# Softmax rows of first and local attention turned by VectorE blocks and DMA, value products behind gates, experts' first slots fetched early

## What is computed

```python
# layers 0, 1
p = softmax(concat([scores_a, sink_col], -1))[..., :-1]
ya = einsum('bnkgqj,bnjkd->bnqkgd', p, va) @ w_proj_a      # first attention, "a"
yb = neighbourhood_attn(qb, kb, vb, rel_bias) @ w_proj_b   # "b"
x = x + (sigmoid(ga) * ya + sigmoid(gb) * yb) @ w_out
# layers 2, 3
y_a = dilated_attention(q_a, k_a, v_a, rel_bias)           # local attention in 256 tokens, "c"
y_m = sigmoid(z_m) * norm(mlstm_chunkwise(q_m, k_m, v_m, i_pre, log_f))
merged = g_a * (y_a @ w_br_a) + g_m * (y_m @ w_br_m)       # g_*: sigmoid(x @ w_gate + b_gate)
y = sum(gate[..., e] * swiglu(x, w13[e], w2[e]) for e in range(8))   # layer 3
```

## Time and profile before

| | before |
|---|---|
| median of 3 timed runs | 2236.96 us (2236.05 to 2237.69) |
| profiled execution | 2238.39 us |
| its span, first to last instruction | 2237.0 us |
| mean granted TensorE clock | 0.998 |
| PE busy | 2217.7 us, 99% |
| DVE busy | 1760.3 us, 79% |
| ACT busy | 1364.5 us, 61% |
| POOL busy | 167.5 us, 7% |
| DMA | 611.39 MB, mean 273 GB/s |

### The profile page before, as it was taken

The page is one execution under the profiler, slowest core; times in us unless marked ns, Lnnn a source line. Parts: engine busy times, 40 slices in busy tenths (PEclk is TensorE's granted clock), DMA queues, the critical chain, the costliest instruction groups (busy, mean ns, idle before and its releaser), DMA issues.

```text
span 2237.0 us, 30263 instructions
## 1 busy us (share of the span) xinstructions
PE 2217.7 (99%) x12156; PEld 1904.7 (85%) x12156; DVE 1760.3 (79%) x2253; ACT 1364.5 (61%) x1764; POOL 167.5 (7%) x231
## 2 busy tenths in 40 slices
PE   9999999999999999999999999999999999999997
PEld 7998888998888999888899887888888888888886
DVE  7976656977564588665678898999999998989898
ACT  5654444655443454444455577777777777877775
POOL 3100111300120000211100010000000000000001
PEclk9999999999999999999999999999999999999999
DMA  8455764546763535776625699999999999999996
GB/s 279 151 191 212 240 233 154 176 170 215 246 235 132 185 132 208 245 236 205 226 93 187 249 349 406 386 380 388 376 382 382 386 370 386 373 392 360 390 372 251
DMA packets 104163, 611.39 MB, mean 273 GB/s; under 512 B 24056, under 2 KB 25384, under 8 KB 34896
## 3 DMA queue, kind: packets, MB, share of 16 engines
q1 hardware_dynamic: 80496, 568.76, 67.3%
q0 software_dynamic: 9872, 31.12, 4.0%
q10 hardware_dynamic: 13648, 9.50, 1.6%
HBM read 591.07 MB, written 18.62 MB: 273 GB/s over the span
## 4 chain that ended last, share of the span: by engine, by line
PE 96%; DVE 3%; DMA 1%; ACT 0%; issue 0%; SPq 0%; POOL 0%; DVEq 0%
PE bank L491 28%; PE bank L493 28%; PE bank L492 28%; PE bank L488 8%; DVE wl L1662 2%; PE bank L768 1%; PE bank L721 1%; PE bank L521 1%; DMA spare<-in_ws 1%; DMA raw<-in_ws 0%; PE bank L816 0%; PE bank L1088 0%; DVE TU L1873 0%; DVE EL L1689 0%; ACT wh L1189 0%
## 5 line engine op out<-in xcount | busy, mean ns | idle before, releaser
L1662 DVE TENSOR_TENSOR wl<-raw,wh 128x1024 fp32r<-128x1024 f32 x698 | 819.9, 1223 | 219.9 <-ACT wh L1189 216.7
L1189 ACT ACTIVATE wh<-raw 128x1024 fp32r<-128x1024 f32 x704 | 704.3, 1052 | 331.1 <-PE bank L493 295.2
L491 PE MATMUL bank<-wh,GH 128*128 128x512 f32 x896 | 352.8, 394 | 0.0
L493 PE MATMUL bank<-wh,GL 128*128 128x512 f32 x896 | 349.3, 390 | 0.0
L492 PE MATMUL bank<-wl,GH 128*128 128x512 f32 x896 | 348.8, 389 | 0.0
L1662 DVE TENSOR_TENSOR wl<-spare,wh 128x1024 fp32r<-128x1024 f32 x264 | 309.8, 1221 | 26.8 <-ACT wh L1189 25.3
L1189 ACT ACTIVATE wh<-spare 128x1024 fp32r<-128x1024 f32 x264 | 264.2, 1054 | 61.0 <-PE bank L493 56.9
L491 PE MATMUL bank<-HH,wh 128*128 128x256 f32 x832 | 239.6, 288 | 0.1
L492 PE MATMUL bank<-HL,wh 128*128 128x256 f32 x832 | 235.3, 283 | 0.0
L493 PE MATMUL bank<-HH,wl 128*128 128x256 f32 x832 | 235.2, 283 | 0.0
L491 PE MATMUL bank<-wh,HH 128*128 128x512 f32 (+1 forms) x600 | 223.4, 372 | 0.0
(11 more groups left out here) (319 smaller groups left out, 3537.1 us busy)
## 6 DMA issues: line engine op xcount, KB each, us to landing
raw<-in_ws SPq DMA_DIRECT2D x352, 1024.0 KB, 6.6
spare<-in_ws SPq DMA_DIRECT2D x132, 1024.0 KB, 7.1
more<-in_ws SPq DMA_DIRECT2D x48, 1024.0 KB, 5.0
scratch_blocks<-TB POOLq DMA_DIRECT2D x30, 256.0 KB, 2.9
TURNED<-scratch_blocks POOLq DMA_DIRECT2D x36, 128.0 KB, 4.8
once<-in_ws SPq DMA_DIRECT2D x4, 1024.0 KB, 11.4
scratch_parts<-Y POOLq DMA_DIRECT2D x7, 512.0 KB, 8.5
REL<-in_relb ACTq DMA_DIRECT2D x4, 768.0 KB, 13.3
```

Source lines behind the costliest of these rows:

```text
L491: T.q.matmul(o, l[0], r[0], start=start, stop=False)
L493: return T.q.matmul(o, l[1], r[0], start=False, stop=stop)
L1189: A.q.activation(sets[c % NSET][0][:, half * i:half * i + half], raws[stream.place[n]][:, half * i:half * i + half], ACT.Copy).then_inc(*h ...
L1662: V.q.tensor_tensor(wl[:, half * i:half * i + half], raw[:, half * i:half * i + half], wh[:, half * i:half * i + half].bitcast(f32), ALU.s ...
```

## The change

The rows of "a" and "c" are no longer turned by PE. `v_even_blocks` takes the place of `v_even`: the product by the reciprocal writes PT with the rows arranged in blocks of 32 columns, and two block transposes of 128 x 1024 (128 x 512 for tile 0 of "c") bring them back to LB[t]. `g_turn_p`, on POOL's queue, writes LB[t] to DRAM in two pieces and reads it back in four strided pieces into other buffers: QT (the queries of "a" are through) and PT for "a", LB[t] for "c". `t_block_outputs` reads them in blocks of 32 columns. For "b" the old way stays, but its turned rows land in QBT (by `turned_piece`), and the first half of its queries in QB0.

The value products move behind gates: in layers 0 and 1 tile 0's behind gate 5 and tile 1's behind the second half of gate 6; in layers 2 and 3 tile 0's keep their place behind the first half of gate 2, and tile 1's stand behind the second half of gate 3, whose first half moves ahead of mq and mk. On DVE, `v_gate(l, 1)` of layers 0 and 1 moves behind the block work of tile 0 and the scores of tile 1; ACT's order changes with it. The closing product of a convolution becomes `v_conved`, which stands one convolution later.

For the experts a fifth once buffer is added, and the five are filled as their memory comes free in layer 3 instead of at the router's norm; the load of BIAS moves from `a_router` to behind expert 1's first products, on ACT's queue. The diff, with unchanged lines left out (left out as well: the new semaphores, the declarations of RZX and of the DRAM buffer, the list of five once names and the removal of BIAS's old load):

```diff
@@ -358,8 +360,9 @@
...
-        for i, a in enumerate((0, 2048, 4096, 14336)):
-            raws[f"once{i}"] = at(f"once{i}", a, SLOT)
+        raws["once0"] = nc.alloc_sbuf_tensor_at("once0", [128, SLOT], f32, offset=arena_at + 4 * 22016)
+        for i, a in enumerate((4096, 0, 2048, 14336)):
+            raws[f"once{i + 1}"] = at(f"once{i + 1}", a, SLOT)
...
@@ -412,6 +415,13 @@
...
+        QB0 = U[:, 6656:7168]
+        def turned_rows(a, t):
+            return {"a": (QT[:, 0:2048], PT[:, :]), "c": LB}[a][t]
+        def turned_piece(a, c):
+            return QBT[c // 2][:, 512 * (c % 2):512 * (c % 2) + 512] if a == "b" else PT[:, 512 * c:512 * c + 512]
...
@@ -789,11 +801,27 @@
...
-                        weights_t = PT[:, 128 * n:128 * n + 128]
+                        weights_t = turned_piece(a, n // 4)[:, 128 * (n % 4):128 * (n % 4) + 128]
...
+            ins.then_inc(*groups.fill("to", l, a, t))
+        def t_block_outputs(l, a, t, kts, v, ready, turned=False):
+            room = groups.take(T, "to", l, a, t)
+            P = turned_rows(a, t)[:, 0:1024 * kts].rearrange("p (b x q) -> p x b q", b=4, q=32)
+            T.wait_ge(*p_in[t].at(l, a, 3))
+            for c in range(4):
+                for i in range(kts):
+                    T.wait_ge(*ready(i))
+                    for p in range(2):
+                        weights_t = P[:, (2 * c + p) * kts + i]
+                        if turned:
+                            weights_t = weights_t[:, ::-1, ::-1]
+                        ins = t_mm(room[64 * p:64 * p + 64, 128 * c:128 * c + 128].rearrange("p (b q) -> p b q", b=4),
+                                   v(2 * c + p, i), weights_t, i == 0, i == kts - 1)
...
@@ -856,8 +884,8 @@
...
-                a = 1536 + 256 * (h // 2) + 128 * t
-                return QT[64 * (h % 2):64 * (h % 2) + 64, a:a + 128]
+                a = 256 * (h // 2 % 2) + 128 * t
+                return (QB0 if h < 4 else QT[:, 2048:2560])[64 * (h % 2):64 * (h % 2) + 64, a:a + 128]
...
@@ -874,20 +902,18 @@
...
-            t_turn_p(l, "a", 0, 8, 2, even)
             t_gate(l, 3)
-            t_outputs(l, "a", 0, 2, v_a, lambda i: out("kva", l, i))
             t_scores(l, "b", 0, q_b, k_b, 256, ready_b)
-            t_turn_p(l, "a", 1, 8, 2, even)
             t_gate(l, 4)
-            t_outputs(l, "a", 1, 2, v_a, lambda i: out("kva", l, i))
             t_scores(l, "b", 1, q_b, k_b, 256, ready_b)
             t_gate(l, 5)
+            t_block_outputs(l, "a", 0, 2, v_a, lambda i: out("kva", l, i))
...
             t_gate(l, 6, (0,))
...
             t_gate(l, 6, (1,))
+            t_block_outputs(l, "a", 1, 2, v_a, lambda i: out("kva", l, i))
...
             t_gate(l, 7)
...
@@ -922,9 +948,6 @@
...
-            def even(l, a, t, h):
-                return evened.at(l, a, t, h // 4)
...
@@ -936,12 +959,9 @@
...
-            t_turn_p(l, "c", 0, 8, 1, even)
             t_gate(l, 2, (0,))
-            t_outputs(l, "c", 0, 1, v_c, lambda i: out("v", l, i), True)
-            t_turn_p(l, "c", 1, 8, 2, even)
+            t_block_outputs(l, "c", 0, 1, v_c, lambda i: out("v", l, i), True)
             t_gate(l, 2, (1,))
-            t_outputs(l, "c", 1, 2, v_c, lambda i: out("v", l, i), True)
...
@@ -958,9 +978,10 @@
...
             heads("mv", lambda h: wv[:, h, :], XM, lambda h: out("xm", l, h // 2))
+            t_gate(l, 3, (0,))
             heads("mq", lambda h: wqk[:, h, :], XC, lambda h: xc.at(l, h))
             heads("mk", lambda h: wqk[:, 4 + h, :], XC, lambda h: xc.at(l, h))
-            t_gate(l, 3, (0,))
+            t_gate(l, 3, (1,))
...
@@ -975,7 +996,7 @@
...
-            t_gate(l, 3, (1,))
+            t_block_outputs(l, "c", 1, 2, v_c, lambda i: out("v", l, i), True)
...
@@ -1413,29 +1432,26 @@
...
-            def first_queries():
-                A.wait_ge(*gain.at("qk", 2 * l))
-                a_copy(QT[:, 1536:2048], ("fold", l, "qb", 0), 512, BV[2 * l], True)
-            a_exps(l, "a", 1, 256, True, {3: lambda: a_gate(l, 2), 5: first_queries})
+            a_gate(l, 2)
+            a_exps(l, "a", 1, 256, True)
+            A.wait_ge(*gain.at("qk", 2 * l))
+            a_copy(QB0, ("fold", l, "qb", 0), 512, BV[2 * l], True)
             a_copy(QT[:, 2560:3072], ("fold", l, "kb", 0), 512, BV[2 * l + 1])
-            a_turn_p(l, "a", 0, 8, 2)
...
-            a_turn_o(l, "a", 0, OA[0])
-            a_turn_p(l, "a", 1, 8, 2)
             a_hi(gate_slot(l, 6))
-            a_exps(l, "b", 0, 256)
-            a_gate(l, 4)
-            a_turn_o(l, "a", 1, OA[0])
+            a_exps(l, "b", 0, 256, False, {3: lambda: a_gate(l, 4)})
...
+            a_turn_o(l, "a", 0, OA[0])
+            a_hi(s + MIX)
             a_turn_p(l, "b", 0, 8, 2)
-            a_hi(s + MIX)
+            a_turn_o(l, "b", 0, OB[0])
             a_turn_p(l, "b", 1, 8, 2)
-            a_turn_o(l, "b", 0, OB[0])
...
+            a_turn_o(l, "a", 1, OA[0])
...
@@ -1474,26 +1490,24 @@
...
-            a_turn_p(l, "c", 0, 8, 1)
...
+            a_conv(l, 3)
             a_turn_o(l, "c", 0, OA[1])
-            a_turn_p(l, "c", 1, 8, 2)
             a_gate(l, 2)
-            a_conv(l, 3)
-            a_turn_o(l, "c", 1, OA[1])
...
+            a_gate(l, 3)
             a_copy(VT[:, 0:512], ("mvt", l, 0), 512)
+            a_turn_o(l, "c", 1, OA[1])
...
-            a_gate(l, 3)
...
@@ -1596,6 +1608,10 @@
...
+                if e == 1:
+                    A.wait_ge(*lo_of(EXPERTS + 2).at(EXPERTS + 2, 1))
+                    A.q.dma_start(BIAS[:, 0:2048], bass.AP(ln_d.tensor, 3 * 2048, [[0, 128], [1, 2048]])
+                                  ).then_inc(*ln_in.mark(8))
...
@@ -1997,9 +2013,35 @@
...
+        def v_even_blocks(l, a, t, n):
+            su, kts = sm[f"su{a}{t}"], n // 128
+            turned = PT[:, 0:8 * n].rearrange("p (b r x k) -> p r x b k", b=4, r=2, k=32)
+            for r in range(2):
+                own = slice(4 * r, 4 * r + 4)
+                rz = RZX[:, 8 * r:8 * r + 4 * kts]
+                P = LB[t][:, 1024 * r:1024 * r + 1024]
+                P = P.rearrange("p (x b k) -> p x b k", b=4, k=32) if kts == 2 else (
+                    P.rearrange("p (x b k) -> p x b k", b=8, k=32)[:, :, 0:4])
+                V.wait_ge(*raised.at(l, a, t, 4 * r + 3))
+                if a == "a":
+                    V.wait_ge(*sink_exp.at(l, t))
+                    V.q.tensor_tensor(su[:, own], su[:, own], sm[f"es{a}{t}"][:, own], ALU.add).then_inc(*step.mark())
+                    V.wait_ge(*step.now())
+                V.q.reciprocal(rz.rearrange("p (h i) -> p h i", h=4),
+                               su[:, own][:, :, None].to_broadcast([128, 4, kts])).then_inc(*step.mark())
+                V.wait_ge(*step.now())
+                V.q.tensor_tensor(turned[:, r], P,
+                                  rz[:, :, None, None].to_broadcast([128, 4 * kts, 4, 32]),
+                                  ALU.mult).then_inc(*evened.mark(l, a, t, r))
+            V.wait_ge(*evened.at(l, a, t, 1))
+            for g in range(2):
+                own = slice(4 * n * g, 4 * n * g + 4 * n)
+                V.q.transpose(LB[t][:, own], PT[:, own]).then_inc(*p_blocked.mark(l, a, t, g))
...
-                v_copy(PT[:, 512 * c:512 * c + 512], ("pt", l, a, t, c), 512)
+                v_copy(turned_piece(a, c), ("pt", l, a, t, c), 512)
...
@@ -2077,34 +2119,34 @@
...
             v_scores(l, "a", 0, 256, bias_a(0), sinks)
             v_gate(l, 0)
+            for t in range(2):
+                v_head_norm(l, "b", t)
+            v_even_blocks(l, "a", 0, 256)
+            v_scores(l, "a", 1, 256, bias_a(1), sinks)
             v_gate(l, 1)
-            for t in range(2):
-                v_head_norm(l, "b", t)
-            v_scores(l, "a", 1, 256, bias_a(1), sinks)
-            v_even(l, "a", 0, 256)
-            v_gate(l, 2)
...
-            v_turn_p(l, "a", 0, 8, 2)
-            v_even(l, "a", 1, 256)
+            v_gate(l, 2)
+            v_even_blocks(l, "a", 1, 256)
             v_gate(l, 3)
-            v_turn_o(l, "a", 0, OA[0])
             V.wait_ge(*masked.at(l))
+            V.wait_ge(*p_out[0].at(l, "a", 1))
             v_scores(l, "b", 0, 256, bias_b(0))
-            v_turn_p(l, "a", 1, 8, 2)
-            v_gate(l, 4)
-            v_turn_o(l, "a", 1, OA[0])
+            V.wait_ge(*p_out[1].at(l, "a", 1))
             v_scores(l, "b", 1, 256, bias_b(1))
...
+            v_gate(l, 4)
+            v_turn_o(l, "a", 0, OA[0])
+            v_turn_p(l, "b", 0, 8, 2)
             v_even(l, "b", 1, 256)
-            v_turn_p(l, "b", 0, 8, 2)
             v_gate(l, 5)
+            v_turn_o(l, "b", 0, OB[0])
+            v_turn_p(l, "b", 1, 8, 2)
             v_gate(l, 6)
-            v_turn_p(l, "b", 1, 8, 2)
-            v_turn_o(l, "b", 0, OB[0])
+            v_turn_o(l, "a", 1, OA[0])
+            v_turn_o(l, "b", 1, OB[0])
             v_gate(l, 7)
-            v_turn_o(l, "b", 1, OB[0])
...
@@ -2121,6 +2163,9 @@
...
```

(41 more changed lines are left out.)

15 lines of the change are left out of this document (8 added, 7 removed).

## The result

The changed kernel takes 2246.28 us (median of 5 timed runs, 2245.39 to 2248.34) against 2236.96 of the kernel before (5 runs beside it, 2236.05 to 2239.69): ratio 1.0043, 95% interval 1.0031 to 1.0055. It is slower by 9.3 us where 6.3 were forecast (2243.3 us). The profiled execution has a span of 2244.1 us, 7.1 more than before.

What follows compares the result with a forecast made beforehand. PE was taken as the bound, busy 2217.7 of 2237.0 us, with DVE level in first-layer attention. Layers 0 and 1 -1.1, layers 2 and 3 +4.8, clock +2.6: +6.3 on the median 2236.96 gives 2243.3 us, range 2234 to 2250.

Steps and rivals of the forecast that it cites:

- What PE loses: Softmax-row transposes leave PE: 3.44 us in each of layers 0 and 1, 2.58 in each of 2 and 3, 12.0 in all.
- Layers 0 and 1: PE waits 2.1 us at gate 3 and 0.8 for ACT against 3.44 saved; both layers give 1.1 us.
- The wait for ACT: Layers 0 and 1, local attention: ACT's first copy of turned rows at 119.9, PE wants it at 119.1; wait 0.8 us.
- Layers 2 and 3: PE waits 5.0 us for gate 3's low parts against 2.58 saved; each layer 2.4 us longer, both 4.8.
- the other moved steps have room: Layers 0 and 1: low parts of gates 4, 5, 6 ready near 95.3, 103, 113.4, wanted at 98.6, 106.6, 116.0.
- The clock: After one of the two 5.0 us waits PE's clock falls once, costing 2.6 us; bounds nothing and 3.7.
- the forecast family: Case A, chance 0.60: 2240.7 us without a clock fall (0.15), 2243.3 with one (0.28), 2245.9 with two (0.17).
- the one with two falls: The clock falls after both 5.0 us waits of layers 2 and 3: 2245.9 us, chance 0.17.
- DMA and queues: Rows written to DRAM and read back on POOL's queue return in some 20 us, the tightest has 27; cost 0.
- the rival of late rows: Descriptors held up by DVE make rows return late, beyond 27 us; at 30 us the time is 2249.3; chance 0.03.
- Experts' first slots: Early fetch of the experts' first weight slots gains 0; bound -2.3 us, the whole PE hole near 1357.
- Sum: Span 2237.0 - 1.1 + 4.8 + 2.6 = 2243.3 us; +6.3 on the timed median 2236.96 gives 2243.3.

Runs made afterwards that it cites:

- e9_slot3_l01: Changed kernel, layers 0 and 1: DVE makes gate 3's whole slot before tile 1's scores, ACT copies folded queries and keys before tile 1's exponentials; 2246.54 us, ratio 1.0040.
- e8_slot3_l23: Changed kernel, layers 2 and 3 alone: DVE makes gate 3's whole slot right behind the second convolution; 2235.57 us, ratio 0.9993 to the kernel before.
- e7_l01_only: Changed kernel with layers 2 and 3 put back as in the kernel before; 2237.86 us, ratio 1.0001 to the kernel before.

## Why the prediction was right, point by point

- **What PE loses.** 12.0 us forecast; 112 transposes went, and the products on blocks take 1.97 us for 32, as in rows. The two groups of layer 2 stood for 2.51 us in the trace of before, where the sum has 2.58. Right.
- **Layers 0 and 1.** The wait ahead of gate 3: 2.1 forecast, 2.11 measured, with its end at 90.74 against 90.6 for the low parts. The wait for ACT: 0.8 and 0.59. Both layers: -1.1 and -1.3. The block transposes took 1.22 each, between the 1.14 taken and the bound of 1.42. That the second wait is not independent of the first, but catches whatever the first lets go (run `e9_slot3_l01`), was not in the working; it did not matter for the sum, and would have for a mend.
- **Layers 2 and 3.** The wait: 5.0 forecast, 4.53 measured. DVE's steps from the end of the normalisation to gate 3's slot took 15.9 us (785.08 to 800.93, below), where the sum had 16.4; the wait for ACT was 0.63 for the 0.8 of the sum, and the waits for tanh went as said. A second and smaller wait was missed: 0.42 us at 839 and again in layer 3, 0.6 each from start to start and 0.7 with the slower products behind it. The step that failed is the one that said that the other moved steps have room: it was worked out for gates 4 to 6 of layers 0 and 1 and not for the mLSTM's rows, which PE now reaches earlier relative to DVE. ACT's copy of them (838.63) stands behind its exponentials, which waited for DVE's maxima until 836.2. The wait stayed at 0.43 in the runs where the one ahead of gate 3 is gone. The timeline of DVE in layer 2 after:

```profile
785.08 2.37 DVE L2040 STREAM_TRANSPOSE L<-PT 128x1024 f32<-128x1024 f32 x2
...
798.86 0.69 DVE L1705 TENSOR_TENSOR OAL<-bank,OAH 128x512 fp32r<-128x512 f32 x1 [0.63 <-ACT OAH L1223]
...
800.93 3.49 DVE L1678 TENSOR_TENSOR wl<-raw,wh 128x1024 fp32r<-128x1024 f32 x3
```
- **The clock.** Here two errors cancel, and that is luck. The sum took one fall at 2.6 us; there were two, at 1.5 and 1.3, 2.8 together. At the price of the sum two would have given 2245.9, and of the three cases of the forecast family the one with two falls had 0.17. The bounds of nothing and 3.7 per fall held. The reading behind the term, that the clock falls some 4 us after PE has stopped and that a wait must be about that long, doesn't hold. Behind the twelve waits of 4.1 to 4.5 us in six traces the clock always fell, between 2.7 and 5.3 us after PE had stopped, and in three of them it stayed at 0.50 for 6.8 us instead of 3.4. It can fall behind the waits of 2.1 us as well, which was said of no case: none in the profile of the changed kernel, one in layer 1 in three other runs and one in each of layers 0 and 1 in a fourth, five in fourteen such waits, each worth 0.8 us once the wait for ACT has given its part back. In all five PE was already at work again when the clock fell. Such falls would account for the timed median standing 2.2 us further from the one before than the span does. The mean granted clock of each timed run points the same way: 0.995 and 0.996 in the two runs of the changed kernel above 2248 us, 0.996 and 0.997 in the other three; and of the ten runs of `e8_slot3_l23` 0.998 in the two shortest (2233.24 and 2233.71), 0.996 or 0.997 in the other eight. Where the clock fell is seen in the profiled runs alone, so this is argued and not shown. The Trainium skill, TensorE: Matmul & The Clock Gate, Part 1, has an idle array fall to the 1.2 GHz level and only activity bring it back; the stretch of 3.4 us at half the clock beside a working PE, and its absence with the filler, agree.
- **DMA and queues.** A return was put at 20 us; tile 1's in layer 0 took about 12: its rows were turned at 100.8, 512 KB out landed in a median of 3.7 us, the four issues back took from 105.7 to 107.9, and such a piece landed in a median of 5.5. No wait of PE or DVE names it. Cost 0 was right, and the rival of late rows was not near. The warning of the Trainium skill, SBUF — State Buffer, on how DVE blocks a DMA issued from POOL showed in none of these transfers, beside a DVE that was busy all the time. The page ties it to DVE's 2-port perf-mode instructions, and no row here tells whether any of these ran in that mode.
- **Experts' first slots.** 0 forecast, 0 shown by the run without them.
- **Sum.** Span +6.3 forecast, +7.1 measured. The difference of 0.8: the mLSTM's values +1.4, the rest of the experts +0.4, clock +0.2, transposes of layers 2 and 3 +0.1, the waits of layers 2 and 3 ahead of gate 3 -0.6 (4.7 each from start to start), layers 0 and 1 -0.2, the hole at the experts -0.6. So the waits carry the result as forecast, and the closeness of the sum owes something to terms that cancel. In the timed medians, +9.3, the forecast is 3.0 short.

## What to carry to other kernels

Where PE is busy 99% of the time and DVE is level with it, taking work from PE pays only after the order of the engine behind it has been redone: follow each operand that PE will reach earlier (weights, banks, copied rows) back to the instruction that makes it, and move that one too. An idle wait of a few us can cost more than its length, since the clock may fall behind it (here 1.3 to 1.5 us for waits of 4.5); a filler shows how much. And when a slot or tile is split in halves, look which index the halves cut, on the producer's side and on the consumer's, before moving one half.

## What the runs showed of the hardware

Idle times of 4.1 to 4.5 us were followed in every trace by a granted clock of 0.50, for 3.4 us in nine of twelve cases (a loss of 1.5 and 1.3 us in the changed kernel) and for 6.8 us in three (0.7 to 1.4 us more from gate 3 to the next wait in these layers). Idle times of 2.1 us were followed by 3.4 us at 0.50 in five of fourteen cases and by 1.00 in the others, at the same place of the same instructions (443 to 446 us: 1.00 in the changed kernel, 0.51 in `e7_l01_only`). 19 dummy products (38 instructions) in the idle time kept the clock at 1.00. DVE's transpose of 32 x 32 blocks costs the same as a product of the same size (1.224 against 1.225 us for 128x1024). The Trainium skill, VectorE: DVE Perf Modes, The three transpose paths, says that it turns blocks of 32 x 32 only and warns of a DMA that does the turning by strides; here the DMA moves whole runs of a block row, 256 KB pieces of which landed in 5.2 and 5.5 us (medians for the two tiles of layer 0), so the warned case is not what these runs show.
